# A two-layer hybrid encoder trunk: the opening's transfers and zero products, dt ahead of the norm, and the inverse root by logarithm and exponent

## The reference, cut to what matters

```python
for l in range(2):
    h = rms_norm(x, norm_mix_g[l])            # x * rsqrt(mean(x*x) + 1e-6) * g
    aq, ak, av, rq, rk, rv, rg, sz, sxbc, sdt = jnp.split(h @ w_in[l], offs, axis=-1)
    ya = swa_sink_attention(aq, ak, av, ...)  # 8 heads, window of 128
    yr = retention(rq, rk, rv, rg, ...)       # 4 heads
    ys = ssd_mixer(sz, sxbc, sdt, ...)        # depthwise conv of 4 taps, softplus(sdt), scan
    x = x + jnp.concatenate([ya, yr, ys], axis=-1) @ w_out[l]
    h = rms_norm(x, norm_ffn_g[l])
    x = x + conv_ffn(h, ...)                  # two 1024 x 2816, conv of 3 taps, one 2816 x 1024
return rms_norm(x, final_norm_g)
```

## Time and profile before

| | us |
|---|---|
| median of three runs | 1277.07 (1276.74 to 1277.92) |
| the profiled execution | 1277.31 |
| its span, first to last instruction | 1275.5 |
| mean granted clock of TensorE | 0.998 |
| PE busy | 1259.7 (99%) |
| DVE, ACT, POOL busy | 640.6, 565.8, 589.3 |

### The profile page before, as it was taken

How to read it: one execution, slowest core, us unless ns; L and a number is a source line. 1 busy time by engine, 2 the same in 40 slices (tenths; PEclk the granted TensorE clock), 3 DMA queues, 4 the chain that set the end, 5 groups by cost and what they waited for, 6 DMA issues and landing times.

```text
span 1275.5 us, 21088 instructions
## 1 busy us (share of the span) xinstructions
PE 1259.7 (99%) x6070; PEld 1026.6 (80%) x6070; DVE 640.6 (50%) x965; ACT 565.8 (44%) x904; POOL 589.3 (46%) x439
## 2 busy tenths in 40 slices
PE   9999999999999999999999999999999999999996
PEld 6887778888888888888878887788888888888884
DVE  6859774565454013342368697646645430133423
ACT  5542584564333224443335237764643432344433
POOL 4543442535545445554445335325454444455541
PEclk9999999999999999999999999999999999999999
DMA  7353222334333333333333522213233333333333
GB/s 218 103 152 103 70 59 66 91 84 115 99 92 98 99 96 94 99 94 88 101 84 94 164 67 84 83 50 104 84 111 96 94 99 99 92 98 98 93 96 110
DMA packets 77771, 124.89 MB, mean 98 GB/s; under 512 B 7912, under 2 KB 20744, under 8 KB 77704
## 3 DMA queue, kind: packets, MB, share of 16 engines
q1 hardware_dynamic: 76936, 122.81, 33.7%
q10 hardware_dynamic: 768, 1.23, 0.3%
HBM read 121.45 MB, written 2.55 MB: 97 GB/s over the span
## 4 chain that ended last, share of the span: by engine, by line
issue 41%; PE 36%; POOL 20%; POOLq 2%; ACT 1%; DMA 1%; DVE 0%; SPq 0%; ACTq 0%; DVEq 0%
PE dense L1128 35%; POOL w_lo L406 19%; PE mix L1128 1%; POOLq L405 1%; POOLq L419 1%; DMA x<-in_xT 1%; DVE arena L1119 0%; PE mix L1465 0%; ACT h_hi L459 0%; POOL sq L438 0%; ACT arena L498 0%; ACT L481 0%; ACT L478 0%; ACT w_hi L507 0%; POOL wdt_g L428 0%
## 5 line engine op out<-in xcount | busy, mean ns | idle before, releaser
L406 POOL TENSOR_TENSOR w_lo<-w_raw,w_hi 128x512 fp32r<-128x512 f32 x424 | 579.6, 1382 | 651.3 <-ACT w_hi L522 648.1
L1128 PE MATMUL dense<-h_hi,w_hi 128*128 128x512 f32 x992 | 390.4, 394 | 1.3 <-ACT w_hi L507 0.7
L1128 PE MATMUL dense<-h_lo,w_hi 128*128 128x512 f32 x992 | 386.3, 390 | 0.0
L522 ACT ACTIVATE w_hi<-w_raw 128x512 fp32r<-128x512 f32 x422 | 257.6, 627 | 286.4 <-PE dense L1128 264.5
L1128 PE MATMUL dense<-h_hi,w_lo 128*128 128x512 f32 x992 | 269.7, 389 | 0.0
L1128 PEld LDWEIGHTS dense<-h_hi,w_hi 128*128 128x128 f32 x992 | 186.4, 188 | 42.9 <-issue 2.9
L1128 PEld LDWEIGHTS dense<-h_hi,w_lo 128*128 128x128 f32 x992 | 186.2, 188 | 40.5 <-issue 1.7
L1128 PEld LDWEIGHTS dense<-h_lo,w_hi 128*128 128x128 f32 x992 | 186.6, 188 | 39.7 <-issue 1.4
L1128 PE MATMUL dense<-m_hi,w_hi 128*128 128x512 f32 x544 | 212.9, 391 | 0.0
L1128 PE MATMUL dense<-m_lo,w_hi 128*128 128x512 f32 x544 | 211.8, 389 | 0.0
L1128 PE MATMUL dense<-m_hi,w_lo 128*128 128x512 f32 x544 | 147.7, 389 | 0.0
(11 more groups left out here) (212 smaller groups left out, 1188.0 us busy)
## 6 DMA issues: line engine op xcount, KB each, us to landing
w_raw<-in_w SPq DMA_DIRECT2D x424, 256.0 KB, 2.7
arena<-cum_rows SPq DMA_DIRECT2D x8, 512.0 KB, 6.1
x<-in_xT SPq DMA_DIRECT2D x8, 256.0 KB, 7.4
out_y<-arena SPq DMA_DIRECT2D x8, 256.0 KB, 2.2
arena<-exp_rows SPq DMA_DIRECT2D x12, 128.0 KB, 6.4
w_raw<-in_w ACTq DMA_DIRECT2D x4, 256.0 KB, 6.1
consts<-in_consts SPq DMA_DIRECT2D x1, 643.0 KB, 4.1
rel_scratch<-arena SPq DMA_DIRECT2D x1, 382.0 KB
```

Source lines behind the costliest of these rows:

```text
L406: nc.gpsimd.tensor_tensor(w_lo[:, s, :], w_raw[:, s, :], w_hi[:, s, :].bitcast(f32), ALU.subtract).then_inc(lo_ready, 1)
L522: nc.scalar.activation(w_hi[:, slot, :], w_raw[:, slot, :], ACT.Copy).then_inc(hi_ready, 1)
L1128: return T.matmul(dst, lhsT, rhs, start=start, stop=stop)
```

## The change

In the opening, SP issues the norm weights ahead of x0, and takes pack 3 and the late parameters from ACT, behind x7. ACT issues `rel`, then pack 0, loads the Silu table, and only then issues packs 1 and 2. The zero products are nine instead of six. In `SCHEDULE` DT stands ahead of NORM, which moves it on PE (the only engine that does something in both). In NORM, ACT calls `rms`, the helper of the other norms, in place of the `Sqrt`; it signals `rstd_ready`, and DVE's reciprocal and its wait for the root fall away. The reload of the Silu table stays behind it.

```diff
--- before.py
+++ after.py
@@ -32,7 +32,7 @@
 SLOTS = 4
 POOL_SQUARES = 2
 FIRST_LOADS = "x0 w0 x1 w1 x2 x3 w2 x4 x5 w3 x6 x7".split()
-WARM = 6
+WARM = 9
 
 
 
@@ -90,7 +90,7 @@
 
 
 SCHEDULE = (
-    "G0 G1 G2 G3 H0 H1 NORM DT L0 U0 DX L1 U1 L2 L3 TT TK D4 U2 DTB D5 D6 DTC U3 CR D7 CX D8 CM BC TOL D9 SA0 D10 D11 SB0 SA1 "
+    "G0 G1 G2 G3 H0 H1 DT NORM L0 U0 DX L1 U1 L2 L3 TT TK D4 U2 DTB D5 D6 DTC U3 CR D7 CX D8 CM BC TOL D9 SA0 D10 D11 SB0 SA1 "
     "GQ0 GQ1 GQ2 GQ3 SB1 SA2 LQ0 QE0 LQ1 QE1 LQ2 QE2 LQ3 QE3 SB2 SA3 GV0 GV1 AS0 GV2 GV3 SB3 AE0 AX0 "
     "LV0 VE0 LV1 VE1 LV2 VE2 AT0 AS1 LV3 AE1 VE3 D20 AX1 AV0 D21 ZM0 ZM1 AT1 AS2 AE2 D22 AX2 AV1 SN0 ZM2 "
     "D23 AT2 SX0 ZM3 AS3 AE3 D24 AX3 AV2 SN1 D25 SX1 D26 AT3 D27 AV3 "
@@ -323,10 +323,11 @@
 
         @block.sync
         def _(sp):
-            sp.dma_start(x[:, 0, :], a["xT"][0]).then_inc(x_loaded[0], 16)
             sp.dma_start(p_all[:, 0:G_COLS], a["params"][:, 0:G_COLS]).then_inc(g_loaded, 16)
-            for i in range(1, KD):
+            for i in range(KD):
                 sp.dma_start(x[:, i, :], a["xT"][i]).then_inc(x_loaded[i], 16)
+            sp.dma_start(w_raw[:, SLOTS - 1, :], a["w"][SLOTS - 1]).then_inc(raw_loaded[SLOTS - 1], 16)
+            sp.dma_start(p_all[:, G_COLS:], a["params"][:, G_COLS:]).then_inc(p_loaded, 16)
             sp.dma_start(wdt_raw[:, :], a["wdt"]).then_inc(wdt_loaded, 16)
             sp.dma_start(c_all[:, 0:EARLY], a["consts"][:, 0:EARLY]).then_inc(c_loaded, 16)
 
@@ -483,12 +484,11 @@
             def gcol(e, o):
                 return par["g"][:, bass.ds(e * KD + o, 1)]
 
+            act.dma_start(ar("relh")[0:32, :], a["rel"]).then_inc(rel_loaded, 16)
             act.dma_start(w_raw[:, 0, :], a["w"][0]).then_inc(raw_loaded[0], 16)
-            act.dma_start(ar("relh")[0:32, :], a["rel"]).then_inc(rel_loaded, 16)
-            for i in range(1, SLOTS):
+            nc.scalar.preload_act_table(ACT.Silu)
+            for i in range(1, SLOTS - 1):
                 act.dma_start(w_raw[:, i, :], a["w"][i]).then_inc(raw_loaded[i], 16)
-            act.dma_start(p_all[:, G_COLS:], a["params"][:, G_COLS:]).then_inc(p_loaded, 16)
-            nc.scalar.preload_act_table(ACT.Silu)
             act.wait_ge(g_loaded, 16)
             def first_square(o):
 
@@ -541,9 +541,7 @@
                 for name in SCHEDULE:
                     step, n = step_of(name)
                     if step == "NORM":
-                        act.wait_ge(m_ready[1], ready(name, 0, l))
-                        nc.scalar.activation(rstd[:, :], M[1][:, :], ACT.Sqrt, scale=1.0 / D,
-                                             bias=par["eps"][:, 0:1]).then_inc(m_free[1], 1)
+                        rms(0, name, l)
                         nc.scalar.preload_act_table(ACT.Silu)
                     elif step == "G":
                         hi_to(SLOTS + n)
@@ -811,8 +809,6 @@
                     step, n = step_of(name)
                     if step == "U":
                         if n == 0:
-                            dve.wait_ge(m_free[1], ready("NORM", 0, l) + 1)
-                            V.reciprocal(rstd[:, :], rstd[:, :]).then_inc(rstd_ready, 1)
                             dve.wait_ge(rstd_ready, l * 2 + 1)
                         dve.wait_ge(run_done, l * N_SEGS + (SEG0 + UNIT_END[n]))
                         row = pad[:, CONV_ORDER.index(n) % 2, 3:3 + S]
```

## The result

The changed kernel takes 1278.7 us (median of 20 runs, 1276.82 to 1281.52) beside 1277.09 us before (20 runs, 1275.49 to 1278.38): a ratio of 1.0013, 95% interval 1.0007 to 1.0019. It is 1.6 us slower, which is less than the 0.2% of the prediction, so "no difference" by that bound; but the time lies above the forecast of 1276.0 and above the range of 1274.4 to 1277.7. The profiled execution took 1278.93 us with a span of 1277.1, which is 1.6 more than the 1275.5 of before. Only the profiled execution of each version has a trace.

What follows compares the result with a forecast made beforehand. TensorE, busy 1259.7 of 1275.5 us, was taken as the bound. The opening's 1.7 us gain less 0.64 us lost at the norms gave 1.1 us, so 1276.0 us against the median of 1277.07, range 1274.4 to 1277.7.

Steps and rivals of the forecast that it cites:

- (b): Opening, nine zero products: the whole first pack runs at the upper clock, 2.72 instead of 4.54 us, gain 1.82 us.
- (a): Opening, new order of first transfers and table load: first product 0.2 us earlier, ends 0.48 us earlier and 0.3 us late.
- the third rival: More than the sum: slow products vary by run, transfers advance ACT, norms cost nothing; 2.7 us faster, 1274.4 us; chance 12%.
- late next: Opening, after a fast first pack: PE stalls 0.1 us for w_lo1 and 0.2 us for w_hi7 and h_lo7.
- (c): Norm of each layer, dt moved ahead of it: costs PE nothing itself, but ACT's start comes 1.86 us later.
- (d): Norm of each layer, root by logarithm and exponent: 2.66 instead of 4.20 us to DVE's unit 0, gain 1.54 us per layer.
- The sign named for this: Norm, in the changed profile: DVE's unit 0 starts 2.8 us after L0's start on PE, instead of 2.45.
- The rule on the tables: Norm, ScalarE: logarithm then exponent cost one table load; unit 0 would be 1.28 us earlier per layer, no wait at TT.
- the clock does not follow: First rival, first pack: it stays slow, the opening gives only 0.2 us, the norms cost 0.64; 1277.5 us; chance 25%.
- The second: Rival, norms: no wait at TT, by a shared table or shorter DVE chain; opening's 1.7 stays whole, 1275.4 us; chance 15%.
- the fourth: Rival, opening: w1 or w3 lands after ACT wants it; with w3 3.5 us late, 1278.6 us; chance 6%.
- The bound of 1.3 for TT: Norms, worst end: twice the booked 0.64 us loss, if DVE's chain in its new place meets POOL's work.

Runs made afterwards that it cites:

- e13: Kernel before, with only ACT's first two transfers swapped (rel, the bias rows, ahead of w0), six zero products, old norms: 1277.27 us, ratio 1.0004.
- e14: Kernel before, with the norm weights ahead of x0 on SP's queue and rel ahead of w0 on ACT's, six zeros, old norms: 1277.77 us, ratio 1.0007.
- e7: Kernel before, with nine products before the bias product and two behind it, all of ones instead of zeros, leaving no gap: 1276.2 us, ratio 0.9995.
- e9: Kernel before, with the changed kernel's transfers and table load and nine zero products, old norms: 1277.2 us, ratio 0.9997.
- e11: Kernel before, with logarithm and exponent as root (norm still ahead of dt) and nine zero products, old transfers: 1276.05 us, ratio 0.999.
- e5: Kernel before, with nine zero products instead of six and nothing else changed: 1275.78 us, ratio 0.9993.
- e6: Kernel before, with nine zero products, the bias product and two more zero products behind it, leaving no gap: 1276.77 us, ratio 0.9998.
- e12: Kernel before, with logarithm and exponent as root (norm still ahead of dt) and ten zero products, old transfers: 1277.34 us, ratio 0.9997.
- e15: e11 plus the norm weights ahead of x0 on SP's queue and the table load behind ACT's first two issues: 1276.27 us, ratio 0.9993.
- e1: Kernel before, with dt ahead of the norm and logarithm and exponent as root, six zeros, old transfers: 1278.55 us, ratio 1.0016.
- e3: Kernel before, with only dt moved ahead of the norm, square root and reciprocal kept: 1283.84 us, ratio 1.0058.
- e2: Kernel before, with only logarithm and exponent in place of root and reciprocal, the norm still ahead of dt: 1277.06 us, ratio 0.9998.
- e4: Kernel before, with only the changed kernel's transfer order on SP's and ACT's queues and its table load, six zeros: 1277.74 us, ratio 1.0004.
- e10: Kernel before, with dt ahead of the norm, logarithm and exponent as root, and nine zero products, old transfers: 1277.41 us, ratio 1.0004.

## Why the prediction was wrong, point by point

The measured 1278.7 is 2.7 us above the forecast. 2.1 of this is the opening, booked as 1.7 earlier and measured 0.42 later, and 0.5 is TT, booked as 0.64 and measured as 1.18. The step that failed is (b): the clock's full gain of 1.82 us was taken as sure, and in after's profile it is nothing.

- **(a), x0 landing: failed.** "At worst h_hi starts at 5.15 (gain 0.03 us)" took the measured latency of x0 plus its later issue as the worst case. It started at 5.47, because x0 landed 0.75 us later, not 0.45 at most. (The bad end of 0.3 us in (a) was for a late w1, which did not come.) The step looked at each queue alone; e13 and e14 show that it takes small transfers at the head of both. The rest of (a) held: the table and the norm weights no longer count, and w3 was not late.
- **(b), the clock: the effect exists, its certainty was the error.** Booked was the upper bound, since no row showed "a rise that long activity ahead failed to bring". After, e7, e9 and e11 are such rows: PE busy from 1.32 without a break until the bias product ends, and still slow. How often the rise comes early can be estimated from the times: where the norms cost nothing, the profiled executions whose whole first pack ran fast took 1275.59 to 1276.07 (e5, e6, e12, e15), those with a slow one 1276.76 and more. In e5 and e11, 14 of 22 runs are below 1276.1; of the 140 of before, with six zeros, 24. So nine zeros make the fast pack more frequent, worth 1.4 us in e5's median. The spread of the runs agrees with the rule cited, that the number of slow products differs from run to run (the Trainium skill, TensorE: Matmul & The Clock Gate, Part 1). The prediction gave it one sentence and a place in the third rival, and should have taken part of the gain instead of all. What the prediction had as late next can't show in after, which has no fast pack, but it does in others: w_lo1 costs the booked 0.1 us in e5, and at pack 7 PE waits for w_hi in e15 (0.40 us) and for h_lo in e12 (0.31), while in e5 it waits for neither.
- **(a) and (b) together: not foreseen.** e9 has both and is 1277.2 where e5 is 1275.78. Their intervals overlap, so the counts have to speak: below 1276.1 are one of e9's 11 runs and six of the 11 of e11, timed beside it; of after's 20, with 1.18 for TT taken off, one. So with the new order the early rise is rare even with nine zeros. How is open: in all nine traces with nine or ten zeros the bias product already tells what the pack will be (0.48 to 0.49 us and fast, or 0.80 and slow), when nothing of the later x0 has reached PE. An idle stretch that ends a rise, as in e13, could be it, but no trace with nine zeros shows such a fall in the opening.
- **(c) and (d): the mechanism right, its size wrong.** The wait at TT came in both layers, at the place named, with the price of PE idle one for one. Predicted was 1.86 - 1.54 = 0.32; measured 0.59. dt's slot: from H1's last product on PE to ACT's start 23.11 to 26.44, 3.33 us, against 1.30 (22.66 to 23.96) before, so 2.03 later and not 1.86; 0.1 of it is that ACT starts 1.16 after the norm's product and not 1.06. Logarithm to unit 0: 26.44 to 29.20, 2.76 and not 2.66. 2.03 + 2.76 - 4.20 = 0.59. Both misses are of a tenth or two, in a difference of two larger numbers. The sign named for this, unit 0 2.8 us after the start of L0, came out as 3.36, and 0.32 of that is no lateness: L0 itself starts 2.73 us after H1's last product instead of 3.05. On top, now and then, comes a tail: after has three runs at 1280.02 to 1281.52, e1 four at 1279.96 and above. That it is a fall of the clock behind TT, as in e3, is not shown, as none of them has a trace; their mean clock of 0.994 to 0.996 speaks for it.
- **The rule on the tables** (the Trainium skill, ScalarE: Activation LUTs, Table sets): the trace still disagrees. There is a table load of 1.28 us between logarithm and exponent in the norm too (27.14, above). By the rule TT would not have waited.
- **The rivals.** The first, "the clock does not follow", is the one that after's profile shows: a slow pack, and slower than before. Its time, 1277.5, was too low by the two mis-sized terms: 0.42 later in the opening instead of 0.2 earlier, and 1.18 instead of 0.64 at TT: 1277.07 + 0.42 + 1.18 = 1278.7. The second and third fell; of the fourth a part was right, a transfer in the wrong place, but it was x0 and not w3.
- **The range** ended at 1277.7 because no case joined the failed clock with the upper bounds of (a) and of (c) and (d). The bound of 1.3 for TT was named and then left out of the range. The measured 1.18 is near it, but by luck: its reason, DVE's chain meeting POOL's work, is not what happened.

**The best versions** are e5 (1275.78 us, ratio 0.9993) and e11 (1276.05 us, ratio 0.999): nine zeros, the old order of transfers, the norm ahead of dt. Logarithm and exponent or square root and reciprocal makes no difference that is shown.

## What to carry to other kernels

When a step is moved ahead of a serial chain, the chain pays the whole slot, and a saving inside the chain counts only up to the slack that is left: measure the slack first (e2 shows a gain of 1.23 us that bought nothing), then sum the two edits as one. An order of transfers is to be judged over all queues together, since two changes that do no harm alone can delay the large one behind them. And where the clock's rise is partly chance, one profile shows one draw: book a share of the gain, and put the case where it fails together with the bad ends of the other terms into the range.

## What the runs showed of the hardware that was not expected

- ACT's queue issues transfers while ACT loads a table: the load runs from 1.67 to 2.95, and the issue of w1 and w2 begins at 1.70. The prediction had left that open.
- Whether the clock has risen by the first product differs between executions with the same activity ahead: e5 and after have the same nine zeros and the bias product from 5.44 or 5.46, 0.49 us long in the one and 0.80 in the other. Where the bias product takes 0.80 us, the clock rises between 9.6 us (e2) and 13.1 us (e4), 3 to 6 us after the first real product. In e10 the nine zeros take 3.79 us and not 4.21: there it rose within the zeros.
- The clock can fall behind a wait of under 2 us: in e3's layer 1 behind 1.86 us of idling and the small products of TT, in e13 behind 1.84, and in e3's layer 0 behind 1.87 it did not. The fall in e3 costs 1.6 us; in e13 the first pack takes 4.27 us instead of the 2.82 of e5.
- The granted-clock column prints 1.00 for the slow products before the first rise (before and after, 6 to 10 us), and 0.50 for those behind a fall (e13, 8 to 11 us). At the start of a kernel the distance between products is the surer sign.
- x0 lands at 3.77 us with a small transfer ahead in ACT's queue alone (one trace), at 4.42 to 4.71 with one in SP's queue alone or in the old order (twelve), and at 5.05 to 5.80 with both (four).
